# Expert-layer kernel: product-key names decoded by two heads, four score buffers, a prefetched attention stage and a three-tile opening

## The chip, the cores and the metric

The kernel runs on one core of one Trainium2 chip. The metric is the device time of one execution in microseconds; the kernel before took 3040.84 us (median of three runs, 3037.55 to 3043.04). A core has TensorE (PE, with its weight loads as PEld), VectorE (DVE), ScalarE (ACT), GpSimd (POOL) and SyncE (SP), each with an instruction queue of its own that is worked off in order, and 16 DMA engines that serve the queues of SP, ACT and POOL.

## The reference, cut to what matters

One decoder layer on 1024 tokens of width 1024: input projections with rotary embeddings, chunked retention and sliding-window attention in blocks of 128 tokens, an output projection with a layer norm, and a product-key expert layer (PEER) with a second norm.

```python
proj = h @ w_in[l]                                  # (1024, 2816)
rq, rk, rv, rg, sq, sk, sv = jnp.split(proj, splits, axis=-1)
...                                                 # rotary, retention, window attention
mix = jnp.concatenate([y_ret, y_swa], axis=-1) @ w_out[l]
h = layer_norm(ALPHA * h + mix, ln1_w[l], ln1_b[l])
ffn = peer_ffn(h, w_pq[l], peer_sub_keys[l], peer_u[l], peer_v[l])
h = layer_norm(ALPHA * h + ffn, ln2_w[l], ln2_b[l])

def peer_ffn(x, w_pq, sub_keys, u_tab, v_tab):      # H = 8 heads, K = 16
    q = (xt @ w_pq).reshape(T, H, 2, PEER_HALF)
    s = jnp.einsum('thpd,hpkd->thpk', q, sub_keys)  # 2 x 128 scores a head
    s1, i1 = lax.top_k(s[:, :, 0], K)
    s2, i2 = lax.top_k(s[:, :, 1], K)
    cand = (s1[..., :, None] + s2[..., None, :]).reshape(T, H, K * K)
    cand_idx = (i1[..., :, None] * PEER_N_KEYS + i2[..., None, :]).reshape(T, H, K * K)
    top_s, pos = lax.top_k(cand, K)
    idx = jnp.take_along_axis(cand_idx, pos, axis=-1)
    g = jax.nn.softmax(top_s, axis=-1)
    ...
    u = jnp.take(u_tab, ib, axis=0)                 # 128 of 16384 experts a token
    a = jax.nn.gelu(jnp.einsum('cd,ced->ce', xb, u), approximate=False) * gb
    return jnp.einsum('ce,ced->cd', a, jnp.take(v_tab, ib, axis=0))
```

## The kernel before, in words

Five stages follow each other, each a block of its own in which every engine has a program; between two blocks all engines meet. A float32 product is made of three: both operands are split into a high part (ACT copies it out as `fp32r`) and a low part (DVE or POOL subtracts), and PE adds high x high, high x low and low x high.

`project` multiplies x by six column chunks of `w_in`, in eight tiles of 128 tokens per chunk; a tile is 8 slices k of three products. Four PSUM banks hold tiles, DVE or ACT empties them into three result buffers and SP stores these to `proj` in DRAM. For the first tile PE waits slice by slice for `x_los` (DVE, L227) and `w_los` (POOL, L204). SP loads the rope tables first (L138), then x and w by slices (L141, L142).

`attend` goes through eight token blocks. Its SP first loads the identity, the `qk` columns of block 0 (L361), five constants (L403), the `v` columns (L366), a norm and `w_out` (L369). PE transposes q and k (L430); DVE and POOL begin when all five constants are there; ACT and POOL split `w_out` between their other work of the first block (L521, L562), and ACT's exponentials (L535) of block 0 are behind them.

`score` forms queries and the 256 key scores of each of 8 heads. DVE searches the top 16 for the token blocks 0 and 1 meanwhile.

`experts_in` computes z for 128 expert tiles on PE (L1139 to L1141): SP loads a tile `u_raw`, ACT copies `u_hi`, POOL subtracts `u_lo` (L823). It runs in 8 steps s of 32 slots k, a tile being two slots. In the steps 0 to 5 DVE searches token block s + 2: in the first 28 slots it works off 32 pieces, eight for each pair q of heads: for each head two sides and the pairs, then piece 6 and piece 7. These last two fall in one slot (6, 13, 20 and 27). After every second pair, piece 6 is `decode` (eight small instructions for four heads, L765 to L772) and `names` for two heads (L780 to L786), and piece 7 `names` for the other two. The scores come from DRAM in two buffers `s_in`, one for each head of a pair; SP waits for a buffer to be read (`s_taken`) before it loads, and the next expert tiles stand behind that on its queue. In every step DVE also takes 34 to 60 dot products with gathered expert rows (L1320), whose gathers POOL issues (L1250) between its splits. From step 2 on DVE makes one-hot rows (`hot`, L1308), ACT scales them (L1181), and PE turns them into gates (L1149) one slot later; there are two `hot` buffers.

`experts_out` adds up a x v in 32 rounds of four expert tiles. Round r + 1 is prepared while r is multiplied: ACT waits for its z and gates, then splits its first `v` tile, and DVE follows. SP's first loads are, in this order, two `v` tiles, h for the blocks that PE cycles through, round 1's z and gates, h for two further blocks and the `v` tiles of round 1. POOL gathers four rows at once.

## Time and profile before

| | |
|---|---|
| median of three runs | 3040.84 us |
| profiled execution, its own time | 3044.0 us |
| its span | 3042.1 us |
| PE, DVE, ACT, POOL busy | 2836.2, 2315.9, 1172.3, 1167.8 us |
| `project`, to its last product | 0 to 265.6 us |
| `attend` and `score` | 265.6 to 743.6 us |
| `experts_in` | 743.6 to 1950 us |
| `experts_out` | 1950 to 3042 us |

The times of the stages are those of the profiled execution, counted from the start of its span. In a row of the timeline the first number is the start, the second the duration, and the square bracket behind it the time for which the engine stood idle before, with what ended that.

### The profile page before, as it was taken

How to read it: one execution, taken by the hardware profiler on the slowest of the kernel's cores; microseconds unless marked ns; L12 is line 12 of the kernel's file. 1: busy time of each engine (PE TensorE's matmuls, PEld its weight loads, DVE VectorE, ACT ScalarE, POOL GpSimd, SP SyncE). 2: the span in 40 equal slices, each digit the busy share in tenths (PEclk: the TensorE clock that was granted, in tenths of full speed). 3: DMA queues.
4: the chain of work that ended last, by engine and by line, in shares of the span. 5: the costliest groups of instructions: out<-in, count | busy, mean ns of one | idle time of the engine just before them, and what ended most of it. 6: DMA issues, size and time to landing. Idle time of an engine off the chain costs nothing. (4 is left out here: it accounts for less than half of the span.)

```text
span 3042.1 us, 42759 instructions
## 1 busy us (share of the span) xinstructions
PE 2836.2 (93%) x15866; PEld 2542.9 (84%) x15866; DVE 2315.9 (76%) x4590; ACT 1172.3 (39%) x2215; POOL 1167.8 (38%) x878
## 2 busy tenths in 40 slices
PE   7997898999689999999999999979999999999998
PEld 6886786888689999999999999868888888888886
DVE  4214776375999998989898777378888888888887
ACT  2112232222112466666666767423333333333331
POOL 3222221000466544444445655333333444444431
PEclk9998999999889999999999999989999999999999
DMA  4223321222689777777777999799999999999991
GB/s 163 93 88 129 105 87 70 81 73 83 217 278 302 267 262 259 270 262 262 265 261 270 361 371 362 268 321 315 333 329 314 325 335 312 326 337 310 331 324 70
DMA packets 310474, 744.35 MB, mean 245 GB/s; under 512 B 22416, under 2 KB 136464, under 8 KB 307088
## 3 DMA queue, kind: packets, MB, share of 16 engines
q0 software_dynamic: 92160, 335.59, 30.8%
q1 hardware_dynamic: 189968, 307.74, 30.3%
q10 hardware_dynamic: 28160, 98.58, 8.1%
q8 instruction: 113, 1.85, 0.2%
q14 instruction: 73, 0.60, 0.1%
HBM read 623.33 MB, written 118.49 MB: 244 GB/s over the span
## 5 line engine op out<-in xcount | busy, mean ns | idle before, releaser
L1529 PE MATMUL y_ps<-v_hi,a_hi 128*128 128x512 f32 x1536 | 600.6, 391 | 25.4 <-DVE a_lo L1671 18.7
L1530 PE MATMUL y_ps<-v_lo,a_hi 128*128 128x512 f32 x1536 | 600.0, 391 | 0.0
L1531 PE MATMUL y_ps<-v_hi,a_lo 128*128 128x512 f32 x1536 | 599.8, 391 | 0.0
L823 POOL TENSOR_TENSOR u_lo<-u_raw,u_hi 128x1024 fp32r<-128x1024 f32 x128 | 308.0, 2406 | 612.9 <-ACT u_hi L819 612.6
L1139 PE MATMUL z_first<-hT_hi,u_hi 128*128 128x384 f32 x1024 | 360.5, 352 | 49.7 <-POOL u_lo L823 44.7
L1599 POOL DMA_INDIRECT v_rows<-in_v,room x176 | 235.6, 1339 | 340.4 <-DVE y L1654 323.4
L1529 PEld LDWEIGHTS y_ps<-v_hi,a_hi 128*128 128x128 f32 x1536 | 289.9, 189 | 86.8 <-DVE a_lo L1671 19.3
L1140 PE MATMUL z_first<-hT_lo,u_hi 128*128 128x384 f32 x1024 | 350.9, 343 | 0.0
L1141 PE MATMUL z_first<-hT_hi,u_lo 128*128 128x384 f32 x1024 | 350.1, 342 | 0.0
L1530 PEld LDWEIGHTS y_ps<-v_lo,a_hi 128*128 128x128 f32 x1536 | 289.9, 189 | 60.4
L1531 PEld LDWEIGHTS y_ps<-v_hi,a_lo 128*128 128x128 f32 x1536 | 289.8, 189 | 60.5
L1181 ACT ACTIVATE hot_g<-hot,gT 128x128 f32<-128x128 f32 x768 | 244.2, 391 | 142.7 <-DVE hot L1308 125.2
L1139 PE MATMUL z_rest<-hT_hi,u_hi 128*128 128x256 f32 x1024 | 296.7, 290 | 0.0
L1141 PE MATMUL z_rest<-hT_hi,u_lo 128*128 128x256 f32 x1024 | 289.3, 282 | 0.0
L1140 PE MATMUL z_rest<-hT_lo,u_hi 128*128 128x256 f32 x1024 | 289.2, 282 | 0.0
L1654 DVE SCALAR_TENSOR_TENSOR y<-v_rows,a_rows,y 128x1024 f32<-128x1024 f32 x176 | 225.6, 1282 | 58.5 <-DMA v_rows<-in_v,room 54.6
L1308 DVE TENSOR_TENSOR hot<-near,iT 128x1024 f32<-128x1024 f32 x192 | 233.7, 1221 | 43.7 <-PE g_ps L1149 43.2
L1564 ACT ACTIVATE v_hi<-room 128x1024 fp32r<-128x1024 f32 x128 | 135.8, 1061 | 325.9 <-DMA room<-in_v 322.9
L1149 PE MATMUL g_ps<-hot_g,hot 128*128 128x128 f32 x1536 | 210.9, 283 | 50.4 <-ACT hot_g L1181 43.5
L1149 PEld LDWEIGHTS g_ps<-hot_g,hot 128*128 128x128 f32 x1536 | 197.9, 197 | 56.0 <-ACT hot_g L1181 45.8
L1139 PEld LDWEIGHTS z_first<-hT_hi,u_hi 128*128 128x128 f32 x1024 | 200.1, 195 | 51.3 <-POOL u_lo L823 46.1
L1320 DVE CUSTOM_DVE_ANT_0 room<-room,h_ps 128x1024 f32<-128x1024 f32 x161 | 196.3, 1219 | 33.3 <-DMA room<-in_u,room 21.4
(213 smaller groups left out, 6006.0 us busy)
## 6 DMA issues: line engine op xcount, KB each, us to landing
u_raw<-in_uT SPq DMA_DIRECT2D x128, 512.0 KB, 4.4
room<-in_v SPq DMA_DIRECT2D x128, 512.0 KB, 7.0
gates<-g_sb ACTq DMA_DIRECT2D x24, 2048.0 KB, 9.9
z<-z_sb ACTq DMA_DIRECT2D x128, 320.0 KB, 6.3
g_in<-gates SPq DMA_DIRECT2D x16, 1536.0 KB, 18.9
room<-gates SPq DMA_DIRECT2D x15, 1536.0 KB, 18.9
room<-z SPq DMA_DIRECT2D x16, 1280.0 KB, 7.1
z_in<-z SPq DMA_DIRECT2D x16, 1280.0 KB, 8.1
```

The source lines that it names most:

```text
L823: self.nc.gpsimd.tensor_tensor(self.u_lo[e][:], self.u_raw[e][:], self.u_hi[e][:].bitcast(F32), ALU.subtract).then_inc(self.u_lo_in[e], 1)
L1139: nc.tensor.matmul(o, u_hi[e][:, k], hT_hi[:, k, cols], start=(k == 0), stop=False)
L1140: nc.tensor.matmul(o, u_hi[e][:, k], hT_lo[:, k, cols], start=False, stop=False)
L1141: last = nc.tensor.matmul(o, u_lo[e][:, k], hT_hi[:, k, cols], start=False, stop=(k == KT - 1))
L1149: last = nc.tensor.matmul(g_ps[g][:, t], hot[g][:, 1, t], hot1_g[g][:, t], start=True, stop=True)
L1181: last = nc.scalar.activation(hot1_g[g][:, t], hot[g][:, 0, t], ACT.Copy, scale=gT[:, t0 + t:t0 + t + 1])
L1308: nc.vector.tensor_tensor(hot[g][:], bc(bc(iota_ps, 1, 4), 1, 2), bc(iT[:, :, t0:t0 + 4], 3, NK), ALU.is_equal).then_inc(hot_in[g], 1)
L1529: nc.tensor.matmul(o, ah, v_hi[p][:, i, c], start=(opens(r, s) and i == 0), stop=False)
L1530: nc.tensor.matmul(o, ah, v_lo[p][:, i, c], start=False, stop=False)
L1531: last = nc.tensor.matmul(o, al, v_hi[p][:, i, c], start=False, stop=(closes(r, s) and i == GROUP - 1))
L1599: nc.gpsimd.indirect_dma_start(out=rows_in[i % RING][:], out_offset=None, in_=d["u"] if table == "u" else d["v"].rearrange("a b c -> (a b) ...
L1654: nc.vector.scalar_tensor_tensor(y[:, b], rows_in[i % RING][:], a_rows[:, b, slot:slot + 1], y[:, b], ALU.mult, ALU.add).then_inc(row_used, 1)
```

## The change

Four edits, and what they need.

`project` is begun by three tiles at once: x comes in two halves of 512 tokens, the first half and w slice by slice, then the rope tables, then the second half; PE takes slice k of the tiles 0, 1 and 2 before slice k + 1. `x_raw` lies in the area that later stages use for prefetched data (`room`), so that the rows for the first attention block and the identity are loaded inside `project`.

In `TopK`, `decode` takes two heads instead of four, and stands before each `names`: piece 6 of every pair of heads is `decode`, piece 7 `names`. In `score` the same is done after every second head instead of every fourth.

`s_in` has four buffers. In `experts_out`, round 1's z and gates are loaded before the h blocks, and POOL's first gathers wait until they have landed.

```diff
 # project, SP
-                sp.dma_start(rope[:], d["rope"]).then_inc(rope_here, 16)
...
+                for k in range(KT):
+                    sp.dma_start(x_raw[:, k, 0:HALF], d["xT"][:, k, 0:HALF]).then_inc(x_here[k], 16)
+                    sp.dma_start(w_raw[:, k], d["w_in"][:, k, 0:512]).then_inc(w_here[k], 16)
                 sp.dma_start(rope[:], d["rope"]).then_inc(rope_here, 16)
                 sp.dma_start(rope64[:], d["rope64"]).then_inc(rope_here, 16)
                 for k in range(KT):
-                    sp.dma_start(x_raw[:, k], d["xT"][:, k]).then_inc(x_here[k], 16)
-                    sp.dma_start(w_raw[:, k], d["w_in"][:, k, 0:512]).then_inc(w_here[k], 16)
+                    sp.dma_start(x_raw[:, k, HALF:T], d["xT"][:, k, HALF:T]).then_inc(x_rest_here, 16)
+                sp.dma_start(room.ident[:], d["ident"]).then_inc(room.ident_here, 16)
...
+                    if (c, tb) == (len(chunks) - 1, 4):
+
+                        sp.wait_ge(x_los, 2 * KT)
+                        for i in range(OUT):
+                            sp.wait_ge(stored[i], 16 * len(range(i, n - 3, OUT)))
+                        for here, both in ((room.qk_here, (slice(0, 2 * RW), slice(4 * RW, COLS - SKV))),
+                                           (room.v_here0, (slice(2 * RW, 4 * RW), slice(COLS - SKV, COLS)))):
+                            for cols in both:
+                                sp.dma_start(room.pj[:, cols], proj[0][:, cols]).then_inc(here, 16)
 # project, PE
+                for k in range(KT):
+                    for n in range(WAVE):
+                        slice_of(n, k)
+                for n in range(WAVE, len(tiles)):
                     if n >= NB:
                         pe.wait_ge(*finished(n - NB))
                     for k in range(KT):
...
+                        slice_of(n, k)
 # attend, SP
-                sp.dma_start(ident[:], d["ident"]).then_inc(ident_here, 16)
-                load_qk(0)
                 for t, n in ((zeta, "zeta"), (xi, "xi"), (decayT, "decayT"), (masks, "masks"), (sinks, "sinks")):
                     sp.dma_start(t[:], d[n]).then_inc(const_here, 16)
-                load_v(0)
                 sp.dma_start(gn_w[:], d["gn_w"]).then_inc(norm_here, 16)
 # TopK
-        pos = self.pos[:, b % 2, half * PH // 2:(half + 1) * PH // 2]
+        pos = self.pos[:, b % 2, 2 * two:2 * two + 2]
 # score, DVE
-                    if h % 4 == 3:
-                        tk.decode(link, b, h // 4)
-                        for two in range(2):
-                            tk.names(link, b, h // 4 * 2 + two)
+                    if h % 2:
+                        tk.decode(link, b, h // 2)
+                        tk.names(link, b, h // 2)
 # experts_in, SP and DVE
-                            wait(sp, s_taken[j], m)
+                            x = 2 * (m % 2) + j
+                            wait(sp, s_taken[x], m // 2)
...
-                    elif n == 6 and q % 2:
-                        tk.decode(link, b, q // 2)
-                        tk.names(link, b, q - 1)
-                    elif n == 7 and q % 2:
+                    elif n == 6:
+                        tk.decode(link, b, q)
+                    elif n == 7:
                         tk.names(link, b, q)
...
                 for b in range(2):
-                    tk.decode(link, b, 1)
-                    for two in range(Q // 2, Q):
-                        tk.names(link, b, two)
+                    tk.decode(link, b, Q - 1)
+                    tk.names(link, b, Q - 1)
 # experts_out, SP and POOL
                 load_v(0, first=2)
+                load_z(1)
                 load_h(slice(GB + 1, TB - 1), cycled_here)
-                load_z(1)
...
                     if r == 0:
+                        pool.wait_ge(z_here[1], 32)
                         for k in range(EARLY):
                             gather(k)
```

Where the rows of an engine's program stand shows in the order in which the two kernels issue them. SP's queue at the start of `project`, before:

```order
L138 DMA rope<-in_rope 128x1024
L139 DMA rope<-in_rope 128x512
L141 DMA x_raw<-in_xT 128x1024
L142 DMA w_raw<-in_w_in 128x512
L141 DMA x_raw<-in_xT 128x1024
L142 DMA w_raw<-in_w_in 128x512
```

And now, from the last two of eight pairs with which it begins (`room` is x's new place):

```order
L142 DMA room<-in_xT 128x512
L143 DMA w_raw<-in_w_in 128x512
L142 DMA room<-in_xT 128x512
L143 DMA w_raw<-in_w_in 128x512
L144 DMA rope<-in_rope 128x1024
L145 DMA rope<-in_rope 128x512
L147 DMA room<-in_xT 128x512 x8
L148 DMA ident<-in_ident 128x128
L154 DMA w_raw<-in_w_in 128x512 x8
L157 DMA proj<-res 128x512 x8
```

The pairs have moved ahead of the rope tables, x's second half and the identity behind them. SP's queue from the last chunk of `project` into `attend`, before:

```order
L151 DMA proj<-res 128x256 x8
L134 UNCONDITIONAL_BRANCH
L354 UNCONDITIONAL_BRANCH
L400 DMA ident<-in_ident 128x128
L361 DMA room<-proj 128x1024
L361 DMA room<-proj 128x640
L403 DMA zeta<-in_zeta 128x4
L403 DMA xi<-in_xi 128x512
L403 DMA decayT<-in_decayT 128x512
L403 DMA masks<-in_masks 128x512
L403 DMA sinks<-in_sinks 128x8
L366 DMA room<-proj 128x1024
```

The same place now:

```order
L157 DMA proj<-res 128x256 x5
L167 DMA room<-proj 128x1024
L167 DMA room<-proj 128x640
L167 DMA room<-proj 128x1024
L167 DMA room<-proj 128x128
L157 DMA proj<-res 128x256 x3
L136 UNCONDITIONAL_BRANCH
L391 UNCONDITIONAL_BRANCH
L438 DMA zeta<-in_zeta 128x4
L438 DMA xi<-in_xi 128x512
L438 DMA decayT<-in_decayT 128x512
L438 DMA masks<-in_masks 128x512
```

The four `proj` loads stand ahead of the last three stores, and the constants are the first loads of `attend`. DVE's queue in slot 27 of a step of `experts_in`, from the last instruction of `decode` to the next slot's `hot`, before (`ab` are decoded rows and columns, `found` the names):

```order
L772 TENSOR_TENSOR ab<-ab,past 128x64
L780 TENSOR_TENSOR room<-ab,places 128x1024
L784 TENSOR_TENSOR room<-room,top_i 128x512 x2
L786 TENSOR_REDUCE found<-room 128x2x32
L780 TENSOR_TENSOR room<-ab,places 128x1024
L784 TENSOR_TENSOR room<-room,top_i 128x512 x2
L786 TENSOR_REDUCE found<-room 128x2x32
L1320 ISA room<-room,h_ps 128x1024
L1320 ISA room 128x1
L1308 TENSOR_TENSOR hot<-near,iT 128x1024
```

In the slots 6, 13, 20 and 27 it now stands so:

```order
L806 TENSOR_TENSOR ab<-ab,past 128x32
L813 TENSOR_TENSOR room<-ab,places 128x1024
L817 TENSOR_TENSOR room<-room,top_i 128x512 x2
L819 TENSOR_REDUCE found<-room 128x2x32
L1351 ISA u_rows,room<-u_rows,h_ps 128x1024
L1351 ISA room 128x1
L1339 TENSOR_TENSOR hot<-near,iT 128x1024
```

One `names` has moved from the slots 13 and 27 to the slots 6 and 20, and each has a `decode` of half the width ahead of it.

## Rows read from the trace of the kernel before

**Rows 1.** The page, part 1: busy time, share of the span, instructions.

```profile
PE 2836.2 (93%) x15866; PEld 2542.9 (84%) x15866; DVE 2315.9 (76%) x4590; ACT 1172.3 (39%) x2215; POOL 1167.8 (38%) x878
```

**Rows 2.** PE's waits, whole span: us in total, times, longest us.

```profile
PE z_first L1139 <- POOL u_lo L823: 44.7, 7, 17.2
PE g_ps L1149 <- ACT hot_g L1181: 43.5, 11, 5.4
```

**Rows 3.** Timeline of the opening, by engine: ACT, POOL, PE.

```profile
7.62 1.06 ACT L187 ACTIVATE x_hi<-x_raw 128x1024 fp32r<-128x1024 f32 x1 [5.60 <-DMA x_raw<-in_xT]
...
9.56 1.06 ACT L187 ACTIVATE x_hi<-x_raw 128x1024 fp32r<-128x1024 f32 x1 [0.37 <-DMA x_raw<-in_xT]
...
11.22 25.68 POOL L204 TENSOR_TENSOR w_lo<-w_raw,w_hi 128x512 fp32r<-128x512 f32 x15 [0.15 <-ACT w_hi L183]
...
11.21 0.77 PE L171 MATMUL pp<-w_hi,x_hi 128*128 128x512 f32 x1 [11.21 <-POOL w_lo L204]
...
26.72 0.77 PE L171 MATMUL pp<-w_hi,x_hi 128*128 128x512 f32 x1 [0.60 <-POOL w_lo L204]
...
32.40 0.49 PE L172 MATMUL pp<-w_lo,x_hi 128*128 128x512 f32 x1
32.73 0.39 PE L173 MATMUL pp<-w_hi,x_lo 128*128 128x512 f32 x1
32.96 0.40 PE L171 MATMUL pp<-w_hi,x_hi 128*128 128x512 f32 x1
```

**Rows 4.** Timeline of the seam to `attend`, by engine: PE, SP, ACT, DVE, POOL.

```profile
274.74 2.79 PE L430 MATMUL pa<-ident,room 128*128 128x128 f32 x12 [9.11 <-DMA room<-proj]
...
271.36 0.43 SPq L403 DMA_DIRECT2D decayT<-in_decayT  x1
...
280.42 1.06 ACT L521 ACTIVATE wo_hi<-room 128x1024 fp32r<-128x1024 f32 x1 [2.25 <-DMA room<-in_w_out]
...
277.01 0.69 DVE L610 COPY rkT<-pa 128x512 f32<-128x512 f32 x1 [6.86 <-DMA sinks<-in_sinks]
...
281.55 4.69 POOL L562 TENSOR_TENSOR wo_lo<-room,wo_hi 128x1024 fp32r<-128x1024 f32 x2 [1.05 <-ACT wo_hi L521]
```

**Rows 5.** Stretches of `experts_in`: length, busy us by engine, PEclk, DMA share, GB/s.

```profile
743.60:1031.60 288.00, 243.11 (x1561) 241.69 (x1562) 269.62 (x794) 63.62 (x101) 160.52 (x117) 0.91 0.76 259
...
1188.50:1346.00 157.50, 146.04 (x1029) 145.32 (x1028) 143.68 (x363) 99.16 (x209) 72.12 (x51) 0.96 0.75 263
...
1659.50:1804.30 144.80, 142.76 (x1029) 141.68 (x1028) 110.06 (x155) 100.26 (x210) 95.00 (x77) 1.00 0.96 360
```

**Rows 6.** DVE's waits in the step from 1188.5 to 1346.

```profile
DVE hot L1308 <- PE g_ps L1149: 6.3, 6, 4.0
DVE iT L1348 <- PE g_ps L1164: 1.4, 1, 1.4
```

**Rows 7.** DVE's timeline before step 0: a `decode`, a `names`, the next.

```profile
756.00 2.33 DVE L770 TENSOR_TENSOR ab<-ab,step 128x64 uint32<-128x64 uint32 x1
...
769.99 0.19 DVE L765 TENSOR_SCALAR step<-pos 128x64 uint32<-128x64 uint32 x1
...
771.04 0.23 DVE L770 TENSOR_TENSOR ab<-ab,step 128x64 uint32<-128x64 uint32 x1
...
771.83 1.23 DVE L780 TENSOR_TENSOR room<-ab,places 128x1024 f32<-128x1024 uint32 x1
...
775.67 1.23 DVE L780 TENSOR_TENSOR room<-ab,places 128x1024 f32<-128x1024 uint32 x1
```

**Rows 8.** DVE's groups by line, 743 to 1100 us: busy us, mean ns.

```profile
L765 DVE TENSOR_SCALAR step<-pos 128x64 uint32<-128x64 uint32 x7 | 4.6, 662 | 0.0
...
L770 DVE TENSOR_TENSOR ab<-ab,step 128x64 uint32<-128x64 uint32 x7 | 3.7, 525 | 0.2
```

**Rows 9.** Timeline of the last stage's start: ACT, PE.

```profile
1984.15 1.06 ACT L1564 ACTIVATE v_hi<-room 128x1024 fp32r<-128x1024 f32 x1 [18.65 <-DMA room<-in_v]
...
1987.21 0.77 PE L1529 MATMUL y_ps<-v_hi,a_hi 128*128 128x512 f32 x1 [6.72 <-DVE y L1686]
```

More of the change, by code:

```diff
@@ L157, in _, with slice_of @@
             def _(pe):
-                for n, (c, tb) in enumerate(tiles):
+                def slice_of(n, k):
+                    c, tb = tiles[n]
                     w = chunks[c][2]
+                    if c == 0 and tb == TB // 2:
+                        pe.wait_ge(x_los, KT + k + 1)
+                    if tb == 0:
+                        if c == 0:
+                            pe.wait_ge(x_los, k + 1)
+                        pe.wait_ge(w_los, c * KT + k + 1)
+                    xh = x_hi[:, k, tb * P:(tb + 1) * P]
+                    xl = x_lo[:, k, tb * P:(tb + 1) * P]
+                    wh, wl = w_hi[:, c % 2, k, 0:w], w_lo[:, c % 2, k, 0:w]
+                    o = ps[n % NB][:, 0:w]
+                    nc.tensor.matmul(o, xh, wh, start=(k == 0), stop=False)
+                    nc.tensor.matmul(o, xh, wl, start=False, stop=False)
+                    last = nc.tensor.matmul(o, xl, wh, start=False, stop=(k == KT - 1))
+                    if k == KT - 1:
+                        last.then_inc(tile_done, 1)
+                for k in range(KT):
+                    for n in range(WAVE):
+                        slice_of(n, k)
+                for n in range(WAVE, len(tiles)):
                     if n >= NB:
@@ L183, in split_w @@
                     nc.scalar.activation(w_hi[:, c % 2, k, 0:w], w_raw[:, k, 0:w], ACT.Copy).then_inc(w_his, 1)
-                for k in range(KT):
-                    act.wait_ge(x_here[k], 16)
-                    nc.scalar.activation(x_hi[:, k], x_raw[:, k], ACT.Copy).then_inc(x_his, 1)
-                    split_w(0, k)
+                for half in range(2):
+                    t = slice(half * HALF, half * HALF + HALF)
+                    for k in range(KT):
+                        act.wait_ge(*((x_rest_here, 16 * KT) if half else (x_here[k], 16)))
+                        nc.scalar.activation(x_hi[:, k, t], x_raw[:, k, t], ACT.Copy).then_inc(x_his, 1)
+                        if half == 0:
+                            split_w(0, k)
                 for n, (c, tb) in enumerate(tiles):
@@ L721, in __init__ @@
         self.top = sb("top", [P, 2, TOPK])
-        self.ab = sb("ab", [P, 2, PH // 2, TOPK], U32)
-        self.step, self.past = (sb(n, [P, PH // 2, TOPK], U32)[:] for n in ("step", "past"))
+        self.ab = sb("ab", [P, 2, 2, TOPK], U32)
+        self.step, self.past = (sb(n, [P, 2, TOPK], U32)[:] for n in ("step", "past"))
         self.top_i = sb("top_i", [P, 2, 2, PH, TOPK], U32)
@@ L758, in gaps, with decode @@
         return self.nc.vector.tensor_tensor(self.gap[:, b % 2], best, bc(best[:, :, 0], 2, TOPK), ALU.subtract)
-    def decode(self, link, b, half):
+    def decode(self, link, b, two):
         nc = self.nc
-        pos = self.pos[:, b % 2, half * PH // 2:(half + 1) * PH // 2]
+        pos = self.pos[:, b % 2, 2 * two:2 * two + 2]
         row, col = self.ab[:, 0], self.ab[:, 1]
@@ L1019, in experts_in @@
         z_sb = [sb(f"z_sb{e}", [P, ZT]) for e in range(2)]
-        s_in = [sb(f"s_in{j}", [P, 2, NK]) for j in range(2)]
+        s_in = [sb(f"s_in{j}", [P, 2, NK]) for j in range(4)]
         iT, gT = sb("iT", [P, 2, P]), sb("gT", [P, P])
@@ L1038, in experts_in @@
         z_stored = [sem(f"z_stored{e}") for e in range(2)]
-        s_here = [sem(f"s_here{j}") for j in range(2)]
-        s_taken = [sem(f"s_taken{j}") for j in range(2)]
+        s_here = [sem(f"s_here{j}") for j in range(4)]
+        s_taken = [sem(f"s_taken{j}") for j in range(4)]
         gaps, exps = sem("gaps"), sem("exps4")
```

76 lines of the change are left out of this document (37 added, 39 removed).

## The prediction

> **What bounds the kernel now.** I read the page's busy line first, then TensorE's waits over the whole execution, then the timeline where they lie. PE is busy 93% of the span [rows 1], so what can be won is the time in which PE stands still or runs at the lower of its clock levels. The waits [rows 2] name two large holders, both in the experts' first stage: 44.7 us on the split of the next expert tile (`u_lo`) and 43.5 us on the scaled one-hot rows (`hot_g`). The change touches both, and three smaller places: the opening, the seam between projections and attention, and the start of the last stage. For each I ask which engine is late last.
>
> *Opening.* The first x slice can be split at 7.62, later ones follow every 1.94 us (9.56 - 7.62), which for 768 KB is 405 GB/s [rows 3]. PE begins at 11.21. It does three products per slice, waits 0.60 before each new slice, and needs 0.43 us per 512-column product, which is the 1.2 GHz level. The last such gap is at 26.72; from there PE is dense, 13 products later, at 32.40, the pace changes, and from 32.73 a product takes 0.23 us, the 2.4 GHz level. The product at 32.73 is number 36, so 72 products (three tiles) are done at 32.73 + 37 x 0.23 = 41.2.
>
> *Seam.* PE waits 9.11 us for the first `proj` rows, DVE for the last of five constants until 277.01, ACT for `w_out` until 280.42; POOL's four splits start at 281.55 [rows 4], and DVE's last small instructions ahead of ACT's exponentials wait for all four.
>
> *Experts, first stage.* It has eight steps. In the first two (743.6 to 1031.6) DVE is busy 269.6 of 288.0 us; the rest is the gap behind each linked instruction. A step with search and gates takes 157.5 us, the one without search 144.8 [rows 5]. In the 157.5, DVE waits for PE 6.3 + 1.4 = 7.7 us [rows 6], so it needs 149.8. There PE's floor is 144.8 and DVE's 149.8: **DVE is the nearer bound**, and PE's waits on `hot_g` are the form in which it shows.
>
> **The change part by part.**
>
> *Opening.* The rope tables (768 KB) and half of x (256 KB) no longer stand ahead of the first pair: 1 MB at 405 GB/s is 2.6 us, so PE begins at 11.21 - 2.6 = 8.6. The pace of POOL's splits (25.68 / 15 = 1.71 us) and of the loads (512 KB, 1.3 us) stays under the 9 x 0.43 = 3.9 us that nine products need, and under 9 x 0.23 = 2.1 us, so PE is dense from the first slice. I give it the stretch at the 1.2 GHz level of rows 3, 5.7 us and 13 products, then 59 x 0.23 = 13.6: three tiles are done at 27.9, which is 41.2 - 27.9 = **-13.3**. All later tiles follow densely, as now. The extra instructions (eight more ACT copies and DVE subtractions, half as long each) lie beside PE; the second half of x comes 2.8 MB later (7 us) and is wanted only by the fifth tile, after 33. Bounds: -15 (a first pair 2 us earlier still), -1.7 (rival below).
>
> *Seam.* `qk` and `v` rows are loaded from the fifth tile of the last chunk on, under PE's last three tiles. At the new stage's start DVE's constants no longer stand behind the identity and the 832 KB of `qk`: three issues of 0.43 [rows 4] and 2.1 us of transfer, so 3.4 us earlier, at 273.6. From there POOL needed 281.55 - 1.05 - 277.01 = 3.5 us until it could split; `w_out` has another 576 KB less ahead of it, so POOL's own work decides: 277.1 instead of 281.55, and the exponentials behind the four splits move by the same **-4.4**. PE's 9.11 us do not go in full, since DVE's constants are late next. Bounds: 0 (constants as late as now) and -9.1. On SP the four early loads stand ahead of the last three stores; they cost 4 x 0.43 = 1.7 us of issue, which the stage's end would show if it lay on the last store.
>
> *Names by two heads.* A `decode` of 64 columns takes 771.83 - 769.99 = 1.84 us, a `names` 775.67 - 771.83 = 3.84 [rows 7]. A column costs (1.23 - 0.19) / (1024 - 64) = 1.1 ns there, so with 32 columns less each of eight instructions saves 0.035 us: 1.56. Before the steps, two `names` and half of two `decode`s move into the search stage, whose PE does not wait for DVE: 2 x (3.84 + 0.28) = -8.2. Each of the six steps with a search gets four decodes of 1.56 for two of 1.84: +2.6. There are collisions besides: one decode instruction took 2.33 where it takes 0.23, while POOL's split ran [rows 7], and over seven decodes two of the eight instructions averaged 0.66 and 0.53 [rows 8] against 0.19 and 0.23: (0.47 + 0.30) = 0.8 us per decode at least. Four chains of 0.85 the length for two make 1.6 into 2.7: +1.1. So DVE gets 3.7 us per step. First two steps: 2 x 3.7 - 8.2 = **-0.8**. Steps three to six: 149.8 + 3.7 = 153.5, plus what DVE still waits: 7.7 at most, 0 at least. I take 3.4: the 1.4 for the transposed names, and half of the 4.0 at the end, since the burst before it is 1.56 + 3.84 = 5.4 instead of 1.84 + 2 x 3.84 = 9.5 and leaves PE less far behind. 156.9 for 157.5, four times: **-2.4**. Bounds: -5.1 and +3.7 per step.
>
> The Trainium skill, "SBUF — State Buffer", section "Who interferes with whom", says that a DVE instruction with two SBUF inputs and a GpSimd instruction that reads SBUF exclude each other for a whole instruction. By that rule every decode holds four instructions that can be made to wait out a split, and twelve more decodes would pay up to twelve splits. The 2.33 of rows 7 agrees with the mechanism; how often it strikes is another matter, and the averages of rows 8 speak for the smaller sum.
>
> *Four score buffers.* SP may load two rounds ahead, and the expert tiles behind those loads come sooner. Priced at 0: the work that hides it is DVE's, which in the first two steps waits for nothing; PE's wait moves to the next split behind a row gather that DVE has not consumed. If DVE were not full, up to 44.7 us would be open.
>
> *Last stage.* ACT, and DVE behind it, waits 18.65 us for the first `v` tile of round 1, and PE then 6.72 for DVE [rows 9]. The new order puts round 1's z ahead of the h blocks, but both stay ahead of that `v` tile, and so do the bytes. Priced at 0. Bounds: -6.7, and +5.2 if the four first gathers (2 MB at 405 GB/s), now held back until z has landed, all fall into its way.
>
> Sum: -13.3 - 4.4 - 0.8 - 2.4 = -20.9. The profiled execution took 3044.0, 3.2 above the median of 3040.84. 3044.0 - 20.9 = 3023.1; against the median, **3020 us**. A change under 0.2%, 6 us, can't be told from none.
>
> **The rivals.**
>
> *DVE used to the end.* If the shorter bursts leave DVE no wait and no new collision, a step costs 149.8 + 2.6 = 152.4: 4 x -5.1 = -20.4, and the first two steps -3.0. With opening and seam -41: 3000. For it: six waits per step that smoothing can fill. Against it: PE's pace in the last four slots, where DVE has no search left.
>
> *The opening stays slow.* If splits come unevenly and PE keeps gaps, 72 products at 0.43 take 31.0, done at 39.6: -1.6 instead of -13.3, 3032. Against it: nine products per slice cover 1.71 us of split twice.
>
> *Gathers in the way* of the last stage's `v`: +5.2, 3025.
>
> *Every added decode blocked.* If each of the twelve added decodes waits out one whole split of 4.69 / 2 = 2.35 us [rows 4], that is 28 instead of 6 x 1.1 = 6.6: 3020 + 22 = 3042, no change. Against it: the averages of rows 8 are those of about one such wait in seven decodes for each of the two instructions. The Trainium skill's rule, named above, would at its worst give this.
>
> *Four stalls for two* (slower). DVE now bursts in four slots of a step, two of them slots in which it had no search. PE has 144.8 / 32 = 4.5 us per slot. At a burst of 9.5 it stood up to 5.4 [rows 2], so a lead of 4.1 was absorbed, and a burst of 5.4 costs 1.3 while that lead is whole. But DVE's other slots are about as long as PE's; if the lead isn't rebuilt between bursts, each costs 5.4, and the lower clock level behind it 13 x (0.43 - 0.23) = 2.6 more: four times 8 for twice 8 is +16 per step and +64 for four, 3087 with opening and seam. It ends slower from 6 us per step on.
>
> **How the numbers follow.** Forecast 0.62 (its own range 3011 to 3030), DVE used to the end 0.14, opening slow 0.08, gathers 0.08, every decode blocked 0.03, four stalls 0.05. The range, 3004 to 3032, leaves out the low half of the second case and the last two. Faster by over 0.2% (below 3034.8): the first four but for a part of the slow opening, 0.88; within 0.2%, 0.07; slower 0.05.
>
> **What would show it.** After: PE's first product near 8.6, at 0.23 us pace by 15, the 73rd product near 28, the last projection 13 us earlier. In attention, first transposes 1 to 2 us after the stage starts, DVE's first copy still behind a constant, exponentials 17 to 18 us earlier than now. In the experts' first stage four decode groups of 128x32 per step, steps of 155 to 158 us, DVE's busy share unchanged in the first two steps, PE's 17.2 us wait gone but not the sum of such waits. In the last stage ACT still waiting 16 to 20 us for `v`. I am wrong if a step comes under 153 or over 160 us, or if the opening keeps 0.43 us past 20.

## The result, and the profile after

| | before | after |
|---|---|---|
| median, us (13 runs each) | 3039.94 (3035.32 to 3043.04) | 3046.12 (3044.02 to 3049.20) |
| ratio, 95% interval | | 1.0021 (1.0014 to 1.0029) |
| span of the profiled execution, us | 3042.1 | 3046.4 |

The changed kernel is 6 us slower, where I had forecast 20 faster and a range up to 3032. By its profile it wins some 16 us up to the experts' first stage and 4 in that stage's first two steps, and loses 23 in the four steps behind them.

Part 1 of its page [rows 1] and TensorE's waits over the whole span [rows 2] show where to look. The columns of the second are us in total, times, longest.

```profile
PE 2844.5 (93%) x15866; PEld 2550.6 (84%) x15866; DVE 2354.6 (77%) x4726; ACT 1170.4 (38%) x2223; POOL 1159.2 (38%) x878
```

```profile
PE g_ps L1181 <- ACT hot_g L1213: 59.3, 19, 5.9
PE z_first L1171 <- POOL u_lo L856: 37.5, 9, 15.6
```

DVE is busy 38.7 us longer than before for 136 more instructions, 0.28 us each: far more than a decode instruction of 0.19 us costs. The wait on `hot_g` grew from 43.5 to 59.3 us and from 11 to 19 times; that on `u_lo` fell from 44.7 to 37.5, its longest from 17.2 to 15.6.

The opening and the seam, TensorE's timeline (start, length, idle before in brackets) [rows 3, 4]:

```profile
6.58 0.77 PE L186 MATMUL pp<-w_hi,x_hi 128*128 128x512 f32 x1 [6.58 <-POOL w_lo L232]
...
12.94 0.40 PE L186 MATMUL pp<-w_hi,x_hi 128*128 128x512 f32 x1
...
32.85 0.50 PE L186 MATMUL pp<-w_hi,x_hi 128*128 128x512 f32 x1 [1.37 <-DVE res L251]
...
256.62 1.73 PE L464 MATMUL pa<-ident,room 128*128 128x128 f32 x7 [4.61 <-DVE skT L734]
```

The first product stands at 6.58 instead of 11.21. The pace of 0.23 us, the 2.4 GHz level, begins near 13 instead of 32.7, and the 73rd product starts at 25.88 instead of 41.16. At 32.85 there is a stop that I had not foreseen: the fifth tile waits for the bank of the first, because DVE finishes splitting the second half of x (4.91 us, until 28.7) before it turns to results. At the seam the first transposes come at 256.62 for 274.74.

The stages of `experts_in`, cut at the transposed names of each step: length, busy us by engine, granted clock, DMA share, GB/s [rows 5]. The lines are steps 1 and 2, step 5 and step 7.

```profile
727.88:1011.89 284.01, 246.50 (x1561) 244.39 (x1561) 265.16 (x818) 63.67 (x101) 160.64 (x117) 0.91 0.78 263
...
1338.91:1500.49 161.58, 147.21 (x1029) 145.55 (x1028) 149.53 (x378) 98.96 (x209) 71.18 (x51) 0.96 0.71 253
...
1662.93:1808.21 145.28, 143.10 (x1028) 141.63 (x1027) 110.25 (x155) 100.03 (x210) 94.86 (x77) 1.00 0.95 358
```

The step without a search is what it was. Steps 3 to 6, the ones with search and gates, take 161.6 to 163.8 us each and 651.04 together; cut in the same way, those of before take 627.86 (sum rows of the changed kernel, then of the one before):

```profile
sum 651.04, PE 592.79 PEld 585.99 DVE 599.36 ACT 395.37 POOL 283.66; mean PE 148.20 PEld 146.50 DVE 149.84 ACT 98.84 POOL 70.91
```

```profile
sum 627.86, PE 584.92 PEld 582.07 DVE 570.41 ACT 398.10 POOL 287.09; mean PE 146.23 PEld 145.52 DVE 142.60 ACT 99.52 POOL 71.77
```

That is +23.2, 5.8 a step. TensorE's stops in one such step of the changed kernel, the one from 1338.91 (timeline of PE):

```profile
1374.64 1.16 PE L1181 MATMUL g_ps<-hot_g,hot 128*128 128x128 f32 x8 [1.75 <-ACT hot_g L1213]
1410.74 2.08 PE L1181 MATMUL g_ps<-hot_g,hot 128*128 128x128 f32 x8 [5.40 <-ACT hot_g L1213]
1447.57 1.16 PE L1181 MATMUL g_ps<-hot_g,hot 128*128 128x128 f32 x8 [1.63 <-ACT hot_g L1213]
1483.85 2.08 PE L1181 MATMUL g_ps<-hot_g,hot 128*128 128x128 f32 x8 [5.58 <-ACT hot_g L1213]
```

Four stops where before there were two of 5.1 to 5.4, one behind each group of decode and names. Behind the longer ones the eight products take 2.08 instead of 1.05 us: the granted clock had fallen, to 0.50 from 1410.74 to 1414. By its look this is my rival with four stalls. DVE's groups over the four steps say something else. In their rows `room<-ab,places` compares the decoded numbers with the sixteen places, `room<-room,top_i` multiplies by the names (the two make up most of `names`), and `room<-top` adds pairs. First the changed kernel (busy us, mean ns), then the kernel before:

```profile
L817 DVE TENSOR_TENSOR room<-room,top_i 128x512 f32<-128x512 f32 x32 | 38.4, 1240 | 0.6
L783 DVE TENSOR_TENSOR room<-top 128x32 f32<-128x32 f32 x32 | 21.0, 655 | 0.0
L813 DVE TENSOR_TENSOR room<-ab,places 128x1024 f32<-128x1024 uint32 x16 | 19.6, 1225 | 0.5
...
L783 DVE TENSOR_TENSOR room<-top 128x16 f32<-128x16 f32 x96 | 18.0, 242 | 0.0
...
L799 DVE TENSOR_SCALAR step<-pos 128x32 uint32<-128x32 uint32 x16 | 13.9, 869 | 0.0
```

```profile
L780 DVE TENSOR_TENSOR room<-ab,places 128x1024 f32<-128x1024 uint32 x16 | 31.5, 1968 | 0.5
L784 DVE TENSOR_TENSOR room<-room,top_i 128x512 f32<-128x512 f32 x32 | 20.7, 688 | 0.5
...
L749 DVE TENSOR_TENSOR room<-top 128x16 f32<-128x16 f32 x96 | 17.7, 239 | 0.0
L758 DVE TENSOR_TENSOR gap<-best 128x128 f32<-128x128 f32 x4 | 8.9, 2238 | 0.1
L749 DVE TENSOR_TENSOR room<-top 128x32 f32<-128x32 f32 x32 | 8.4, 262 | 0.0
```

The same instruction in the same number costs different sums: the multiplication of names 688 or 1240 ns, the adding of pairs of 32 columns 262 or 655. Three places of one step, POOL's timeline and DVE's, show how:

```profile
1345.40 2.39 POOL L856 TENSOR_TENSOR u_lo<-u_raw,u_hi 128x1024 fp32r<-128x1024 f32 x1 [2.72 <-ACT u_hi L852]
...
1363.19 2.38 POOL L856 TENSOR_TENSOR u_lo<-u_raw,u_hi 128x1024 fp32r<-128x1024 f32 x1 [3.35 <-ACT u_hi L852]
...
1402.68 2.50 POOL L856 TENSOR_TENSOR u_lo<-u_raw,u_hi 128x1024 fp32r<-128x1024 f32 x1 [5.12 <-ACT u_hi L852]
```

```profile
1345.33 2.66 DVE L783 TENSOR_TENSOR room<-top 128x32 f32<-128x32 f32 x4
...
1364.06 1.55 DVE L799 TENSOR_SCALAR step<-pos 128x32 uint32<-128x32 uint32 x1
...
1402.22 3.50 DVE L817 TENSOR_TENSOR room<-room,top_i 128x512 f32<-128x512 f32 x2
```

Each ends within 0.6 us after POOL's split of u ends: 1347.99 behind 1347.79, 1365.61 behind 1365.57, 1405.72 behind 1405.18. Without a split in their way the three take 0.44, 0.17 and 1.29 us, as other instances in the same step do. I call this stretching.

### The profile page after: what moved, and what is told of

It is laid out like the page before. It is cut to its first block and busy times, and to the rows that moved or that the text cites. A ratio compares the mean times of both kernels' runs of the same rounds, so it can differ in the third digit from the quotient of the medians.

```text
span 3046.4 us, 42914 instructions
## 1 busy us (share of the span) xinstructions
PE 2844.5 (93%) x15866; PEld 2550.6 (84%) x15866; DVE 2354.6 (77%) x4726; ACT 1170.4 (38%) x2223; POOL 1159.2 (38%) x878
## 5 line engine op out<-in xcount | busy, mean ns | idle before, releaser
L1559 PE MATMUL y_ps<-v_hi,a_hi 128*128 128x512 f32 x1536 | 600.5, 391 | 27.8 <-DVE a_lo L1702 19.6
L1171 PE MATMUL z_first<-hT_hi,u_hi 128*128 128x384 f32 x1024 | 363.1, 355 | 43.0 <-POOL u_lo L856 37.5
L1181 PE MATMUL g_ps<-hot_g,hot 128*128 128x128 f32 x1536 | 212.6, 284 | 63.4 <-ACT hot_g L1213 59.3
L1351 DVE CUSTOM_DVE_ANT_0 room<-room,h_ps 128x1024 f32<-128x1024 f32 x161 | 196.4, 1220 | 31.2 <-DMA room<-in_u,room 19.4
## 6 DMA issues: line engine op xcount, KB each, us to landing
room<-gates SPq DMA_DIRECT2D x15, 1536.0 KB, 19.5
```

What stands on the lines that cost most here:

```text
L1171: nc.tensor.matmul(o, u_hi[e][:, k], hT_hi[:, k, cols], start=(k == 0), stop=False)
L1181: last = nc.tensor.matmul(g_ps[g][:, t], hot[g][:, 1, t], hot1_g[g][:, t], start=True, stop=True)
L1559: nc.tensor.matmul(o, ah, v_hi[p][:, i, c], start=(opens(r, s) and i == 0), stop=False)
```

## The experiments

Two theories stood after the first look. **Occupancy**: DVE is full in these steps, and every us that it is given, by two more decodes and by stretching, lengthens the step. **Burst**: what counts is how decode and names are bunched, one stop of TensorE for each bunch. A third, that the names are innocent and the four score buffers or the earlier start shift transfers, had to be ruled out first. In the results below "four steps" are steps 3 to 6, and the row is the sum row of the view of stretches: length, then busy us by engine.

### The names back as they were

```diff
...
-                    if h % 2:
-                        tk.decode(link, b, h // 2)
-                        tk.names(link, b, h // 2)
+                    if h % 4 == 3:
+                        tk.decode(link, b, h // 4)
+                        for two in range(2):
+                            tk.names(link, b, h // 4 * 2 + two)
...
-                    elif n == 6:
-                        tk.decode(link, b, q)
-                    elif n == 7:
+                    elif n == 6 and q % 2:
+                        tk.decode(link, b, q // 2)
+                        tk.names(link, b, q - 1)
+                    elif n == 7 and q % 2:
...
```

> The changed kernel with one part undone: the names by four heads at odd q, two at a time behind one decode, as before; the opening, the four score buffers and the last stage's order stay changed. Two theories say the names made steps 3 to 6 longer (occupancy: VectorE, which idles only some 7 to 9 us of a step, got two more decodes and more instructions held up while GpSimd splits u; burst: four slots with decode and names where two were, and TensorE stalls at each). By both the four steps return from 161.6 to 163.8 us to 156.7 to 157.5, which takes off 23.2, and the first two steps lose the 3.8 they won: 3046.1 - 23.2 + 3.8 = about 3027, 0.9957 of before. The rival (the four score buffers or the earlier start shift transfers against the steps, whatever the names do) leaves the steps at 162 to 164 and the time at 3046 or above.

3022.38 us, 0.9949 (0.9935 to 0.9962) of before. The four steps:

```profile
sum 628.05, PE 585.33 PEld 582.50 DVE 570.39 ACT 398.08 POOL 288.31; mean PE 146.33 PEld 145.62 DVE 142.60 ACT 99.52 POOL 72.08
```

628.05 against 627.86 before: without the new names the steps are what they were. The one miss is the first two steps, which I expected to lose 3.8 again; they stay short, 284.17 us from 725.35 on.

### The names alone

The same lines changed in the kernel before, and nothing else.

> The kernel before with one part of the change alone: names by two heads, each two decoded by themselves, in all slots where the changed kernel has them. If the parts add up, steps 3 to 6 come to 161.6 to 163.8 us as in the changed kernel (+23.2 together) and the rest stays as before: 3038 + 23 = some 3061. If the names cost only because the earlier start moved them against GpSimd's splits, the steps stay at 157 to 159 and the time under 3046.

3055.71 us, 1.0063 (1.0048 to 1.0079): slower by 18.7. The four steps take 647.90:

```profile
sum 647.90, PE 589.92 PEld 583.44 DVE 598.75 ACT 396.27 POOL 283.57; mean PE 147.48 PEld 145.86 DVE 149.69 ACT 99.07 POOL 70.89
```

That is +20.0 for the +23.2 of the whole change, so the parts nearly add up, and the earlier start is not what makes the names dear. Here too the first two steps are 3 us shorter (284.68); with the 3.2 that the four steps lack of +23.2 this makes up the difference to 3061.

### Decode and names in slots of their own

```diff
         def pieces_at(k):
-            return range(SLOTS * k // TOPK_SLOTS, SLOTS * (k + 1) // TOPK_SLOTS) if k < TOPK_SLOTS else range(0)
+            if k >= TOPK_SLOTS:
+                return range(0)
+            q, n = k // 7, k % 7
+            return range(8 * q + n + (n > 3), 8 * q + n + 1 + (n > 2))
```

> The changed kernel with the same pieces of the top 16 in the same order, but decode and names no longer in one slot of steps 3 to 6: each has its own, and the slot that holds two pieces now holds two halves of a head's sorting. The work is that of the changed kernel, only the bursts of 5.4 us (3.9 at most now) are gone. Burst theory: TensorE's four stalls a step on hot_g (1.6 to 1.9 and 5.4 to 5.9 us, some 14.8 together) go to under 4, the step to 150 to 153 us, and the time to some 3004. Occupancy theory: VectorE has the same work, the stalls only move, the step stays at 161 to 164 us and the time within 4 us of 3046.

3024.33 us, 0.9954 (0.9939 to 0.9969). Both theories missed: 622.86 for the four steps is 155.7 each, between 150 to 153 and 161 to 164.

```profile
sum 622.86, PE 583.78 PEld 572.22 DVE 581.12 ACT 391.53 POOL 289.49; mean PE 145.95 PEld 143.05 DVE 145.28 ACT 97.88 POOL 72.37
```

The reason is in DVE's groups over them (busy us, mean ns). The work had not stayed the same:

```profile
L813 DVE TENSOR_TENSOR room<-ab,places 128x1024 f32<-128x1024 uint32 x16 | 33.1, 2071 | 0.0
L817 DVE TENSOR_TENSOR room<-room,top_i 128x512 f32<-128x512 f32 x32 | 20.7, 689 | 0.5
...
L799 DVE TENSOR_SCALAR step<-pos 128x32 uint32<-128x32 uint32 x16 | 12.8, 800 | 0.0
L783 DVE TENSOR_TENSOR room<-top 128x32 f32<-128x32 f32 x32 | 6.8, 211 | 0.0
```

The multiplications and pairs that were stretched in the changed kernel are free (38.4 to 20.7, 21.0 to 6.8), and the comparison, free there, is stretched (19.6 to 33.1). These three, with the decode's first instruction (13.9 to 12.8), come to 19.5 us less, 4.9 a step, of the 7.0 by which a step fell. The rest is of the size by which DVE waits less for TensorE before `hot`: 8.3 us over the four steps for 18.3. So this run did not tell the theories apart; it showed that one slot of difference changes which instruction meets a split. In the first two steps, where the same slots changed, it went the other way: they take 292.33 us for 284.01, with DVE busy 273.43 for 265.16.

### Both kernels without the split of u

The split is left out from the third step on in each (`u_lo` keeps an older value, so that the products of those steps are not the reference's), and nothing else is changed.

```diff
...
                     pool.wait_ge(u_hi_in[e], i + 1)
-                    tiles.lo(e)
+                    if whole:
+                        tiles.lo(e)
+                    else:
+                        nc.gpsimd.engine_nop().then_inc(u_lo_in[e], 1)
...
```

> The changed kernel without GpSimd's split of u from the third step of the expert projection on: u_lo keeps what the second step left in it, TensorE multiplies by that, and the output is not the reference's. GpSimd's 2.4 us instructions are gone there, and with them what holds VectorE's instructions on two SBUF operands (7 or 8 of them a step stretched by 1.4 to 2.3 us each, 12.6 to 15.0 together). Occupancy theory: steps 3 to 6 fall by about those 13.8, to 148 to 150 us, where TensorE's own pace (145.3 in step 7) is near; no pairs, names or decode instruction is stretched any more. If the stretching has nothing to do with the split, the rows stay stretched and the steps stay at 162 to 164. Burst theory alone: bursts of 5.4 us remain, four stalls of some 1.6 to 1.9 us each, step at 152 to 154.

> The kernel before with the same omission (no split of u on GpSimd from the third step on; the output is not the reference's). Occupancy theory: the 7.0 us of stretched instructions a step go, steps 3 to 6 fall from 157 to some 150 to 152 us, within 2 us of the changed kernel with the same omission, since without the stretching only two decodes of 1.5 us stand between them. Burst theory: its two bursts of 9.5 us stay the longer ones, stalls of 3 to 5 us each, so that it stays at 154 us or above, and the changed kernel is the faster one of the two by 1 us a step or more.

2984.5 us for the changed kernel and 3014.7 for the one before, one time each. The four steps, first of the changed kernel, then of the one before:

```profile
sum 593.55, PE 576.04 PEld 570.48 DVE 548.71 ACT 397.39 POOL 128.76; mean PE 144.01 PEld 142.62 DVE 137.18 ACT 99.35 POOL 32.19
```

```profile
sum 606.84, PE 579.47 PEld 575.89 DVE 540.88 ACT 396.99 POOL 131.65; mean PE 144.87 PEld 143.97 DVE 135.22 ACT 99.25 POOL 32.91
```

The changed kernel loses 651.04 - 593.55 = 57.5 us of its four steps with the split, 14.4 each; the kernel before 21.0, 5.3 each. Without it the order turns round: the changed kernel's steps are 13.3 us shorter together, 3.3 each. Occupancy had the two kernels within 2 us a step of each other, so it missed there; burst had the kernel before at 154 us or above, where it takes 151.7, and the changed one at 152 to 154, where it takes 148.4. Each theory holds a part: that the shorter bunches help, as the prediction had it, is right, and the stretching outweighs it. DVE's groups of the changed kernel without the split give the undisturbed cost:

```profile
L817 DVE TENSOR_TENSOR room<-room,top_i 128x512 f32<-128x512 f32 x32 | 20.7, 689 | 0.6
...
L783 DVE TENSOR_TENSOR room<-top 128x16 f32<-128x16 f32 x96 | 11.0, 170 | 0.0
L783 DVE TENSOR_TENSOR room<-top 128x32 f32<-128x32 f32 x32 | 5.8, 182 | 0.0
L799 DVE TENSOR_SCALAR step<-pos 128x32 uint32<-128x32 uint32 x16 | 3.2, 200 | 0.0
L792 DVE TENSOR_TENSOR gap<-best 128x128 f32<-128x128 f32 x4 | 1.2, 294 | 0.1
```

### The small operands in PSUM

Leaving the split out proves its price but is no kernel. The cure that leaves all arithmetic in place is to take one operand of each stretched instruction out of SBUF. The hot rows (`hot`), which read `iota` from PSUM, took 1.22 us on average in every kernel, split or not.

```diff
...
+    def to_psum(self, free):
+        self.tops = [free[:, 0:TOPK], self.top[:, 1]]
+        at = TOPK + 2 * PH * TOPK
+        self.top_i = bc(free[:, TOPK:at].bitcast(U32).rearrange("p (a h k) -> p a h k", a=2, k=TOPK), 1, 2)
+        self.ab = free[:, at:at + 4 * TOPK].bitcast(U32).rearrange("p (a h k) -> p a h k", a=2, k=TOPK)
+        self.pos_ps = free[:, at + 4 * TOPK:at + 6 * TOPK].bitcast(U32).rearrange("p (h k) -> p h k", k=TOPK)
...
-        iota_ps = near[:, 0:NK]
+        iota_ps, free_ps = near[:, 0:NK], near[:, NK:512]
...
+                tk.to_psum(free_ps)
                 for s in range(TB):
```

> The changed kernel with the small operands of the names in PSUM from the first step of the expert projection on: one half of a head's top 16, the sixteen's indices, the places and the decoded pair, so that no adding of pairs, no decode and no multiplication of names takes two operands from SBUF; arithmetic, slots and order are those of the changed kernel. Stretching by two SBUF operands: what the run without the split showed comes back with the split in place, no row of pairs, decode or names above 1.4 us an instruction, steps 3 to 6 at 147 to 151 us (there 149.5, 149.9, 147.0, 147.1), the time 3046 - 4 x 14.4 = 2988, less up to 8 in the first two steps, where 24 us are stretched: 2980 to 2990. Rival one (any VectorE instruction that meets the split is held): rows stay stretched, 3040 to 3050. Rival two (the stretching goes, but sorting into PSUM is slower, 0.05 us or more on each of the some 120 sorting instructions a step): steps at 154 to 157, time 3010 to 3020.

2981.69 us, 0.9821 (0.9807 to 0.9834) of before: 55 us faster than before, 64 than the change as it was made. The four steps, and DVE's groups over them:

```profile
sum 601.94, PE 576.66 PEld 570.29 DVE 557.21 ACT 397.38 POOL 282.13; mean PE 144.17 PEld 142.57 DVE 139.30 ACT 99.35 POOL 70.53
```

```profile
L831 DVE TENSOR_TENSOR room<-room,near 128x512 f32<-128x512 f32 x32 | 20.6, 683 | 0.6
...
L785 DVE TENSOR_TENSOR room<-near,top 128x16 f32<-128x16 f32 x96 | 10.5, 165 | 0.0
...
L773 DVE FIND_INDEX8 near<-top,room 128x8 uint32<-128x128 f32 x32 | 9.4, 294 | 0.0
...
L785 DVE TENSOR_TENSOR room<-near,top 128x32 f32<-128x32 f32 x32 | 5.8, 181 | 0.0
L813 DVE TENSOR_SCALAR step<-near 128x32 uint32<-128x32 uint32 x16 | 2.9, 180 | 0.0
```

POOL does all its splits (282.13 us busy, 283.66 in the changed kernel), and these rows of DVE's read as if there were none. Of the four steps the first, 152.16, lies above the 147 to 151 that I expected. The first two steps, where more pairs and names were stretched, fell too, from 284.01 to 268.68 us. Both rivals fall: none of the three groups is held once an operand stands in PSUM, and the search with results in PSUM costs 294 - 285 = 9 ns an instruction, not 50. Of what still reads SBUF alone, the decode's second instruction is now hit: 552 ns on average, for 182 in the run without the split.

### The bunches once more, without stretching

The new `pieces_at` from above, in the kernel with the small operands in PSUM.

> The changed kernel with the small operands in PSUM (which came to 2981.7) and with decode and names in slots of their own, as in the run that moved nothing else (3024.3). There the step had fallen by 6.9 us, and the stretched instructions by 6.3, so that it did not tell bursts from stretching. Here hardly an instruction is stretched (1.2 us a step). Stretching alone: bunching decode and names costs nothing, steps 3 to 6 stay at 149.5 to 152 us and the time within 3 us of 2981.7. Burst: TensorE's stalls of 1.5 and 1.9 us a step (4.8 to 5.9 together) go as well, steps at 146 to 147.5, time 2966 to 2972.

2981.29 us, 0.9819 (0.9806 to 0.9833): no difference to 2981.69. The four steps take 600.54 for 601.94:

```profile
sum 600.54, PE 576.79 PEld 567.60 DVE 559.09 ACT 392.74 POOL 281.83; mean PE 144.20 PEld 141.90 DVE 139.77 ACT 98.18 POOL 70.46
```

The 6.3 us and 1.2 us of stretching in the expectation are too far apart: by the rows it is 4.9 and 1.5. The burst theory, as the account of the loss, falls here: without the stretching, decode and names together in one slot cost nothing that separate slots would save.

### Names by four heads, with operands in PSUM

The first experiment's names with the same move to PSUM, as far as it fits (the places in place of the decoded pairs).

> The changed kernel with the names by four heads as before (3022.4) and with as many of the small operands in PSUM as fit (half of a top 16, the indices, the places, the numbers of the sixteen; the decoded pairs of four heads do not fit). Is the division by two heads worth something once the splits hold little up? Without the split at all the steps were 151 to 152.3 us with four heads and 147 to 149.9 with two. If that carries over: steps 151 to 153.5, time 2995 to 3003, 14 to 21 us behind the 2981.7 of two heads. Rival (the two extra decodes cost what the shorter bursts give): steps at 149 to 150.5 and a time within 4 us of 2981.7.

2998.89 us, 0.9874 (0.9859 to 0.9890), 17 us behind two heads. The four steps:

```profile
sum 612.71, PE 580.17 PEld 576.70 DVE 551.01 ACT 397.26 POOL 281.79; mean PE 145.04 PEld 144.18 DVE 137.75 ACT 99.32 POOL 70.45
```

TensorE waits 28.3 us on `hot_g` in these four, against 18.2 with two heads, and DVE 30.3 for 11.5 on TensorE before `hot`. Stretching doesn't explain the 10.8 us between them: here the gap of the scores is held (8.9 us for 1.2), with two heads the decode's second instruction (8.8 for 2.9). The bunch of a decode and two names does cost more than one of a decode and one names; that was the idea of the change, and it pays as soon as the splits hold little up. The first two steps, 274.73 us for 268.68, are 6 of the 17.

### Two buffers, and the last stage as before

Both on the kernel of the first experiment (3022.38): in one the four score buffers become two again, in the other the second round's z is loaded behind the h blocks again and POOL's wait for it goes.

```diff
-        s_in = [sb(f"s_in{j}", [P, 2, NK]) for j in range(4)]
+        s_in = [sb(f"s_in{j}", [P, 2, NK]) for j in range(2)]
...
```

```diff
                 load_v(0, first=2)
-                load_z(1)
                 load_h(slice(GB + 1, TB - 1), cycled_here)
+                load_z(1)
...
-                        pool.wait_ge(z_here[1], 32)
```

> The changed kernel with the names as before (the run that came to 3022.4) and with two score buffers in place of four as well. That run won 3.6 us in the first two steps of the expert projection (284.2 for 287.8), with the names as before. Theory: the four score buffers gave it, so the two steps go back to 287 to 288 and the time to some 3026. Rival: it comes of the earlier start, so that the two steps stay at 284 and the time within 2 us of 3022.

> The changed kernel with the names as before (3022.4) and with the last stage's second round loaded and its first gathers started as before. My prediction held this part for nothing: then the time stays within 2 us of 3022 and the last stage within 1 us of 1071.3. Rival: the gathers that wait for the second round's load cost the 1 to 2 us by which the changed kernel's last stage is longer (1072.4 for 1070.7): then the last stage comes back to 1069.5 to 1070.5 and the time to some 3020.5.

3023.49 us (0.9958, 0.9943 to 0.9973) and 3022.14 us (0.9954, 0.9938 to 0.9969). Neither part is worth a measurable time. With two buffers the first two steps stay short as well (284.42 us from 725.28 on), so the buffers did not give the 3.6 us.

## Why the prediction was wrong, step by step

*What bounds.* Right in the main: DVE is the nearer bound in steps 3 to 6, and TensorE's waits on `hot_g` are the form in which it shows. With the operands in PSUM DVE is busy 42 us less over the four steps with two heads, and they are 49 us shorter; with four heads 19 and 15. Its busy time alone is not the whole of it: with decode and names in slots of their own DVE was busier than before (581.12 us for 570.41) and the steps were shorter (622.86 for 627.86), since it waited less for TensorE.

*Opening*, -13.3. The mechanism is right. The 73rd product came 15.3 us earlier, since TensorE began at 6.58 and not at 8.6, the fifth tile lost 1.4 of it again, and the last projection product starts at 251.73 for 265.35: -13.6. That this comes within 0.3 of the forecast is luck: an earlier start and a stop, neither of them foreseen, nearly cancel. The pace is at 0.23 us before 15 (in fact by 13), so the rival of a slow opening is out.

*Seam*, -4.4. Mis-sized: where TensorE first waits for `attend`'s own output (`yT_lo`) the lead is 311.19 - 294.89 = 16.3, so the seam gave 16.3 - 13.6 = 2.7. TensorE waits 4.61 us at the start of the stage, then 2.94 for DVE's first copies, and on the exponentials 7.39 for 11.06.

All of the change but the names measures 3022.4 - 3038.0 = -15.6 by time, and 3.6 of that lie in the experts' first two steps; I had -17.7 for opening and seam. The 12 that are left are under the 16.3 of the two profiles; executions of one kernel lie up to 8 us apart (3035.32 to 3043.04), so two profiles can't settle that difference.

*Four score buffers* and *last stage*, 0 each. Right, by the two runs above. The changed kernel's last stage came out 1.7 us longer in its profile, and ACT waits 21.12 us there for `v`, a little over the 16 to 20 I had named; but with and without the new order the stage differs by 0.2 us between the two runs that isolate it.

*Names, first two steps*, -0.8. They became 3.8 us shorter, but they do that with the names as before too (284.17), with two buffers, and with the names alone (284.68); with decode and names in slots of their own they became longer than before the change (292.33). In all of these the length is DVE's busy time and 18 to 19 us more: 269.62 of 288.00 before [rows 5], 265.16 of 284.01, 266.46 of 284.17, 273.43 of 292.33. So what changed is how long DVE was busy. That different instructions meet a split in each order would do this, but no run here isolates it. TensorE's longest wait for the split, which I expected to go, is still there, 15.6 for 17.2.

*Names, steps 3 to 6*, -0.6 each: **this step failed**, at +5.8; all four steps are over the 160 us that I had named as the sign of being wrong. It was a sum of three terms:

| per step | predicted | measured | from |
|---|---|---|---|
| two more decodes | +2.6 | +2.7 | decode groups without the split, 24.2 - 13.4 us over four steps |
| more stretching | +1.1 | +5.2 | below |
| DVE waits less for TensorE | -4.3 | -2.1 | 26.4 + 4.2 before, 18.3 + 4.1 after, over four steps |
| sum | -0.6 | +5.8 | |

The rows behind the third term are DVE's waits before `hot` in the four steps, before and after (us in total, times, longest):

```profile
DVE hot L1308 <- PE g_ps L1149: 26.4, 24, 4.4
```

```profile
DVE hot L1339 <- PE g_ps L1181: 18.3, 5, 4.9
```

The larger miss is the term of stretching, 4.1 us a step, and 2.2 are the waiting; either by itself would have made the step longer than before. I took the stretching from two instructions of a decode [rows 8], 1.6 us a step, and scaled it with the number of decodes. The same view has three more groups that were stretched, a third instruction of the decode among them, and I passed over them:

```profile
L780 DVE TENSOR_TENSOR room<-ab,places 128x1024 f32<-128x1024 uint32 x14 | 22.6, 1617 | 0.5
...
L749 DVE TENSOR_TENSOR room<-top 128x32 f32<-128x32 f32 x22 | 14.2, 645 | 0.2
...
L769 DVE TENSOR_TENSOR ab<-pos,past 128x64 uint32<-128x64 uint32 x7 | 4.4, 627 | 0.2
```

In steps 3 to 6 of the kernel before the stretching was 7.5 a step already: over four steps the comparison 31.5 - 19.6, the two sizes of pairs 17.7 - 10.9 and 8.4 - 5.8, the gap 8.9 - 1.2 and the decode 0.9, together 29.9 us, each against the same row without the split. All of these instructions read only SBUF, and I had priced none but the decodes. In the changed kernel it is 12.7: the multiplications 38.4 - 20.7, the pairs 21.0 - 5.8 and 18.0 - 11.0, the decodes 13.9 - 3.2, together 50.6. In the step from 1338.91 four bunches are held up in place of two, and three additions of pairs in place of one. Which ones meet a split depends on when each falls; the run with decode and names apart shows that one slot shifts it.

The waiting was sized for bunches without stretching, and there it holds: without the split DVE waits 11.4 + 4.2 us for TensorE over the four steps of the changed kernel and 34.9 + 4.1 in the kernel before, 5.9 a step less, and 2.7 - 5.9 = -3.2 is the -3.3 by which its steps are shorter there.

The rival that had this mechanism, every added decode blocked, came nearest: 3042 by 28 us of stretching in the whole stage. That the number comes so near is partly luck: of the 20.7 us of stretching added in the four steps the decodes hold 9.8, and the rest fell on multiplications and pairs. I gave it 3 in 100, because I read two rows of decodes as a rate for the whole search. The rival of four stalls had the right picture, four stops a step and the lower clock behind them, and the wrong cause: with the stretching gone, bunches of a decode and one names are free.

The Trainium skill, "SBUF — State Buffer", section "Who interferes with whom", says that a VectorE instruction with two SBUF inputs and a GpSimd one that reads SBUF, or a `tensor_scalar` in a mode that takes both of VectorE's ports and any GpSimd one, exclude each other for a whole instruction, whichever comes first, and that others with at most one SBUF input are not held. The rows agree as to who is held: the decode's first instruction, a `tensor_scalar`, 869 ns with the split and 200 without, and the multiplication 1240 ns with both inputs in SBUF and 683 with one in PSUM. In which mode the `tensor_scalar` ran no row shows. I had weighed that page's rule against a rate that was drawn from too few rows.

## What to carry to other kernels

When an engine shares something with another, price the sharing over all instructions that can be hit, not over those that the change adds: take each group's mean less its shortest instance, times its count. A rearrangement changes which instructions are hit, so the bound of such a term should be as wide as the whole of it, on both sides; here it was 7.5 us a step before and 12.7 after, and the gain that was sought was 0.6. And where the collision can be removed at its root (a PSUM operand, 384 free words of a bank), do that first: the names by two heads, which cost 24 us (3046.1 against 3022.4), gain 17 once it is done (2981.7 against 2998.9).

## What the runs showed of the hardware that I had not expected

- A split of 2.4 us on GpSimd holds up a small VectorE instruction with its operands in SBUF until it is done: four additions of pairs, 0.44 us, took 2.66, and a `tensor_scalar` of 32 columns 1.55 instead of 0.17. The 16 splits of a step cost 14.4 us of 162.8 in one order of the program and 5.3 of 157.0 in another.
- MAX8 and FIND_INDEX8 on SBUF never showed this (295 and 285 ns, with the split and without), and neither did the reduction of 1024 columns in SBUF (1220 ns in all kernels).
- One operand in PSUM is enough to be free of it (683 ns for 1240), and results of the search written to PSUM cost 9 ns more each (294 for 285).
